# The value product of 16 meta keys: two native fp32 passes against one fp32r product over three stacked 16-row blocks

## The chip, the cores and the metric

The program runs on one core of one Trainium2 chip. The metric is the device time of one execution in microseconds (us); lower is better. TensorE (PE) multiplies, with PEld its weight load; VectorE (DVE), ScalarE (ACT) and GpSimd (POOL) work beside it; SyncE (SP) issues most DMAs. Engines tell each other of finished work by semaphores.

## The reference, cut to what matters

Two transformer blocks follow each other. The change is in the second block, in its two attentions. There 16 learned "meta" tokens stand before 1024 real tokens, so that every query sees 1040 keys.

```python
def second_block(x, meta_tokens, ...):
    h = concatenate([meta_tokens (16 rows), x (1024 rows)])
    z = rms_norm(h) @ w_in                      # qa ka va qb kb vb ga gb
    # A: 8 heads, each of two 64-wide score maps and 128-wide values
    w = softmax(q1 k1^T/8 + alibi) - lam * softmax(q2 k2^T/8 + alibi)
    oa = rms_norm(w @ va)
    # B: 8 query heads over 2 key heads, width 128, rotary positions
    ob = softmax(qh kh^T / sqrt(128)) @ vb
    h = h + (sigmoid(ga) * (oa @ wa) + sigmoid(gb) * (ob @ wb)) @ w_out
    # then 16 experts, each picking its top tokens, and a final norm
```

## The kernel before, in words

**Precision.** Large products are done in split form: each float32 operand is cut into a high part (a copy to the type fp32r) and a low part (operand minus high part, again fp32r), and three fp32r products hi·hi, hi·lo, lo·hi are added. Products with the probabilities are done natively in float32; a native product shows as two MATMUL records, each with its own weight load.

**Tiles.** Queries are taken 128 at a time: eight tiles (t = 0 to 7) of real tokens and a ninth (t = 8) for the 16 meta queries; in B the ninth holds the meta queries of four heads (64 rows). A has 8 × 9 = 72 tiles, B has `NB` = 66 (only the last head of each group has a ninth tile). For one tile:
- PE makes the scores against the 1024 real keys; DVE turns them into biased scores with a row maximum (TENSOR_TENSOR_REDUCE, shown as CUSTOM_DVE_ANT_0; L2579 in A, twice a tile for the two score maps; L2739 in B). The 16 meta scores were made earlier and are only copied in (L2576, L2737).
- ACT exponentiates the row of 1040 (L2176, L2341).
- DVE combines the two maps in A (L2595, "combine") or divides in B (L2746, L2748).
- PE turns the probabilities (L621): first the block of the 16 meta keys into the upper rows' place of bank 7, then the eight blocks of real keys into banks 5 and 6. ACT copies the first out (L2184 in A, L2396 in B) and then the eight (L2189, L2398).
- PE multiplies with the values: eight products over 128 real keys each (L3101, L3298), and one for the meta keys (L3102, L3299). For this last one the 16 rows of probabilities and of values lie in tiles of 128 rows whose other 112 rows are zero, and the product is native like the eight. ACT (L2195) or DVE (L2754, `result_b`) takes the result.

**Order in A.** The order is written out by hand on every engine. In step t of head h PE does: scores of tile t+1; half a unit of the next head's projections (L3037, 12 fp32r products of 348 columns); the turn of tile t; the other half unit; the value products of tile t-1. A unit is one third of the columns of the next head's keys, queries or values (`UNITS`), and the list runs k0 k1 k2 q0 q1 v0 v1 q2 v2 over t = 0 to 8. PE begins unit t+1 only when the results of unit t are out of their bank: for keys that is DVE's `lower_keys` (L2541, L2542). At t = 0 PE turns the head's values (L621 on vTa) after the value products, and it waits there for ACT's copy L2189 of tile 0, which frees banks 5 and 6. At t = 5 and t = 8 the meta scores of the next head follow the value products (L3050). The last head has no units beside it. In a step ACT does: result of tile t-2, exp of map 0, square, copy of the meta block, exp of map 1, copy of the eight blocks, unit.

**Order in B.** In step s PE does: scores of tile s+2 (L3263), half a unit if the step has one (t = 0 to 2 in most heads), the turn of tile s, the other half, the value products of tile s-1. PE turns tile s only when DVE has taken result s-2 out of bank 7. ACT does: meta copy, copy of the eight blocks, exp of tile s+2, unit, and at t = 4 and 5 the high part of the next head's queries (L2332), which DVE follows with the low part (L2716) at the end of its step. At t = 6 of a group's last head the next group's keys are split (L2327, L2729), and the next scores wait for them.

**Weights.** POOL splits each weight tile into its high part (CAST, L655) and low part (TENSOR_TENSOR, L657), started by PE's last use of the slot.

Of the kernel before, what the change touches and what calls it, by code (L numbers as in the profile page):

```python
# [13 lines left out]
P = 128  # L14
# [3 lines left out]
META = 16  # L18
# [104 lines left out]
CREDIT = 1  # L123

# [40 lines left out]
def build(nc, A, out):  # L165

    ctx = ExitStack()
    with ctx:
# [140 lines left out]
        ka_lo[1] = o.put("ka_lo1", [P, TP], F32R)  # L309
        tok_at = (top - 4 * (NT + 1) * D) // 32 * 32  # L310
# [8 lines left out]
        Va_meta = [o.put(f"Va_meta{j}", [P, P]) for j in range(2)]  # L319
        EA = [o.put(f"EA{j}", [P, T2]) for j in range(2)]  # L320
        EA2 = o.put("EA2", [P, T2])
        PTa = [o.put(f"PTa{j}", [P, NT + 1, P]) for j in range(2)]
# [23 lines left out]
        Vb_meta = [o.put(f"Vb_meta{j}", [P, HB]) for j in range(2)]  # L346
        PTb = [o.put(f"PTb{j}", [P, NT + 1, P]) for j in range(2)]
# [86 lines left out]
        def thirds(t):  # L434
# [28 lines left out]
            aa_bias aa_u aa_v aa_vf aa_qs aa_ql aa_kh aa_kl aa_vs aa_s aa_mt aa_ms aa_max aa_e aa_sm aa_c  # L463
# [4 lines left out]
            lg_z lg_c lg_y router_step lg_e lg_t hr_t hr_c tk_step tk_t tk_c  # L468
# [1463 lines left out]
        with nc.Block() as block:  # L1932

            @block.sync
# [205 lines left out]
            def _(act):  # L2140
# [69 lines left out]
                def head(h, odd, first=False, last=False):  # L2210

                    for t in range(NT + 1):
# [6 lines left out]
                        if t == 0:  # L2219
                            act.wait_ge(S["aa_v"], 3 * h + 1)  # L2220
                            act.activation(Va_meta[odd][0:META, :], bank(6, P, 0, META), ACT.Copy).then_inc(S["aa_vs"], 1)
# [160 lines left out]
                for s, (g, j, t) in enumerate(B_TILES):  # L2382
                    m = rows_of(t)
                    after = next_head(g, j)
                    if t == 0 and j == 0:
                        act.wait_ge(S["ob_v"], 3 * g + 1)
                        act.activation(Vb_meta[g][0:META, :], bank(6, P, 0, META), ACT.Copy).then_inc(S["ob_vs"], 1)
# [55 lines left out]
                act.activation(aff[:, :, 0:NE], aff[:, :, 0:NE], ACT.Exp).then_inc(S["lg_e"], 1)  # L2443
# [75 lines left out]
            def _(dve):  # L2519
# [229 lines left out]

                def result_b(s):  # L2750
# [33 lines left out]
                for zeros in (*(t[:, NT, :] for t in PTb), *(t[:, :] for t in Vb_meta)):  # L2784
                    dve.memset(zeros, 0.0).then_inc(S["bb_z"], 1)
                scores_b(1)
                divide(0)
                for s, (g, j, t) in enumerate(B_TILES):
                    after = next_head(g, j)
                    if t == 5 and after:  # L2790
# [62 lines left out]
                dve.wait_ge(S["lg_y"], 1)  # L2853
# [10 lines left out]
                dve.wait_ge(S["lg_e"], 1)  # L2864
# [155 lines left out]
            def _(pe):  # L3020
# [51 lines left out]
                def turn_probs(h, par, t, fresh, more=True):  # L3072
# [8 lines left out]
                    if t == 0:  # L3081
                        pe.wait_ge(S["aa_vs"], 3 * h + 1)
                        pe.wait_ge(S["aa_ms"], 6 * h + 6)
                    if t == 1:
                        pe.wait_ge(S["aa_vs"], 3 * h + 3)
# [10 lines left out]
                def values(h, odd, t, done):  # L3096
# [5 lines left out]
                    mm(bank(7, P, 0, m), PTa[par][:, NT, 0:m], Va_meta[odd][:, :], start=False, stop=True).then_inc(S["aa_o"], 1)  # L3102
# [163 lines left out]
                def turn_probs_b(s):  # L3266
# [11 lines left out]
                    if j == 0 and t < 2:  # L3278
                        pe.wait_ge(S["ob_vs"], 3 * g + (3 if t else 1))
# [10 lines left out]
                def values_b(s):  # L3290
# [3 lines left out]
                    if j == 0 and t == 0:  # L3294
                        pe.wait_ge(S["ob_vs"], 3 * g + 3)
# [3 lines left out]
                    mm(bank(7, m), Vb_meta[g][:, :], PTb[s % 2][:, NT, 0:m], start=False, stop=True).then_inc(S["bb_o"], 1)  # L3299
# [109 lines left out]
                last.then_inc(S["lg_y"], 1)  # L3409
# [157 lines left out]
```

## Time and profile before

| | |
|---|---|
| three runs | 3375.02, 3373.60, 3371.13 us; median 3373.6 |
| profiled execution | span 3371.0 us, 51781 instructions |
| busy | PE 3208.9 us (95%), DVE 1661.5 (49%), ACT 1123.6 (33%), POOL 991.2 (29%) |
| attention A | about 1338 to 1951 us |
| attention B | about 2181 to 2617 us |

The span runs from the first to the last instruction of the profiled execution; the page gives no other time for that execution, and the median of the runs is 2.6 us above it. A row of a timeline gives start, duration, engine, line, operation, tiles, shape and count; a bracket at its end is the idle time of the engine before it and what released it. PE records overlap: the pitch of equal matmuls is (duration of the row − duration of one) / (count − 1).

### The profile page before, as it was taken

How to read it: one execution, taken by the hardware profiler on the slowest of the kernel's cores; microseconds unless marked ns; L12 is line 12 of the kernel's file. 1: busy time of each engine (PE TensorE's matmuls, PEld its weight loads, DVE VectorE, ACT ScalarE, POOL GpSimd, SP SyncE). 2: the span in 40 equal slices, each digit the busy share in tenths (PEclk: the TensorE clock that was granted, in tenths of full speed). 3: DMA queues.
4: the chain of work that ended last, by engine and by line, in shares of the span. 5: the costliest groups of instructions: out<-in, count | busy, mean ns of one | idle time of the engine just before them, and what ended most of it. 6: DMA issues, size and time to landing. Idle time of an engine off the chain costs nothing.

```text
span 3371.0 us, 51781 instructions
## 1 busy us (share of the span) xinstructions
PE 3208.9 (95%) x20325; PEld 2832.4 (84%) x20325; DVE 1661.5 (49%) x2806; ACT 1123.6 (33%) x2092; POOL 991.2 (29%) x672
## 2 busy tenths in 40 slices
PE   7999989899999998999999899999999999789997
PEld 5677767688888877898989799998999999689997
DVE  5555556755554545666666623255455043522223
ACT  3433333333322223555555621155455110300002
POOL 3112224777772333222222133200000222012221
PEclk9999999999999998999999999999999999889998
DMA  4001112122234112000000012100000221468888
GB/s 156 26 32 32 32 63 100 63 75 75 79 108 176 50 53 79 20 26 20 20 20 20 14 44 82 65 25 26 24 22 20 79 90 57 176 224 308 316 306 293
DMA packets 80577, 294.90 MB, mean 87 GB/s; under 512 B 11298, under 2 KB 16226, under 8 KB 77200
## 3 DMA queue, kind: packets, MB, share of 16 engines
q1 hardware_dynamic: 67296, 243.92, 20.4%
q10 hardware_dynamic: 6944, 29.90, 2.2%
q0 software_dynamic: 6160, 18.63, 2.2%
q8 instruction: 122, 2.00, 0.2%
q14 instruction: 55, 0.45, 0.0%
HBM read 239.39 MB, written 47.70 MB: 85 GB/s over the span
## 4 chain that ended last, share of the span: by engine, by line
PE 55%; DVE 3%; issue 2%; ACT 2%; DMA 0%; POOL 0%; SPq 0%; POOLq 0%; DVEq 0%; ACTq 0%
PE PS L633 14%; PE PS L3037 7%; PE PS L3459 7%; PE PS L621 5%; PE PS L3222 4%; PE PS L3489 3%; PE PS L3101 3%; PE PS L3068 3%; PE PS L3298 3%; PE PS L3263 2%; PE PS L3102 0%; PE PS L3050 0%; PE PS L3235 0%; DVE where L2889 0%; DVE affT L2892 0%
## 5 line engine op out<-in xcount | busy, mean ns | idle before, releaser
L655 POOL CAST w_hi<-ring 128x1024 fp32r<-128x1024 f32 x130 | 135.7, 1044 | 1544.6 <-PE PS L633 434.3
L657 POOL TENSOR_TENSOR w_lo<-ring,w_hi 128x1024 fp32r<-128x1024 f32 x130 | 333.0, 2562 | 10.5
L2176 ACT ACTIVATE EA<-EA,small_sb 128x1040 f32<-128x1040 f32 x144 | 166.8, 1158 | 192.2 <-DVE small_sb L2579 192.0
L2579 DVE CUSTOM_DVE_ANT_0 EA<-PS,biasH,low_a 128x1024 f32<-128x1024 f32 x128 | 163.6, 1278 | 57.8 <-PE PS L3068 57.8
L3037 PE MATMUL PS<-u_hi,w_hi 128*128 128x348 f32 x504 | 173.5, 344 | 0.0
L3037 PE MATMUL PS<-u_lo,w_hi 128*128 128x348 f32 x504 | 162.1, 322 | 0.0
L3037 PE MATMUL PS<-u_hi,w_lo 128*128 128x348 f32 x504 | 161.8, 321 | 0.0
L1590 DVE TENSOR_TENSOR hid_lo<-hid,hid_hi 128x1024 fp32r<-128x1024 f32 x44 | 92.7, 2145 | 118.6 <-ACT hid_hi L1222 118.6
L1677 PE MATMUL PS<-u_hi,w_hi 128*128 128x512 f32 x352 | 147.1, 418 | 3.0 <-POOL w_lo L657 2.3
L1871 PE MATMUL PS<-t_hi,slot_hi 128*128 128x512 f32 x352 | 138.7, 394 | 9.4 <-DVE t_lo L1489 8.8
L3101 PE MATMUL PS<-Va,PTa 128*128 128x128 f32 (+1 forms) x1152 | 139.9, 275 | 0.0
L1677 PE MATMUL PS<-u_lo,w_hi 128*128 128x512 f32 x352 | 139.4, 396 | 0.0
L633 PE MATMUL PS<-u_hi,w_hi 128*128 128x348 f32 (+1 forms) x552 | 129.7, 339 | 10.0 <-DVE u_lo L584 3.9
L1677 PE MATMUL PS<-u_hi,w_lo 128*128 128x512 f32 x352 | 138.5, 394 | 0.0
L1871 PE MATMUL PS<-t_hi,slot_lo 128*128 128x512 f32 x352 | 138.5, 393 | 0.0
L1871 PE MATMUL PS<-t_lo,slot_hi 128*128 128x512 f32 x352 | 138.1, 392 | 0.0
L3101 PEld LDWEIGHTS PS<-Va,PTa 128*128 128x128 f32 (+1 forms) x1152 | 133.7, 181 | 3.1 <-issue 1.7
L3298 PE MATMUL PS<-PTb,Vb 128*128 128x128 f32 (+1 forms) x1056 | 128.8, 275 | 0.4 <-DVE obT L2754 0.4
L2595 DVE SCALAR_TENSOR_TENSOR EA<-EA,small_sb,EA 128x1040 f32<-128x1040 f32 (+1 forms) x72 | 127.1, 1765 | 2.5
L633 PE MATMUL PS<-u_lo,w_hi 128*128 128x348 f32 (+1 forms) x552 | 128.0, 335 | 0.0
L633 PE MATMUL PS<-u_hi,w_lo 128*128 128x348 f32 (+1 forms) x552 | 127.7, 335 | 0.0
L3459 PE MATMUL PS<-xsT,w_gate_sb 128*128 128x130 f32 x1024 | 126.9, 277 | 0.6 <-DVE xsT L2927 0.6
(485 smaller groups left out, 8256.6 us busy)
## 6 DMA issues: line engine op xcount, KB each, us to landing
ring<-in_stream SPq DMA_DIRECT2D x130, 512.0 KB, 3.5
w_gate_sb<-in_w_gate SPq DMA_DIRECT2D x64, 512.0 KB, 7.3
w_up_sb<-in_w_up SPq DMA_DIRECT2D x64, 512.0 KB, 8.2
w_down_sb<-in_w_down SPq DMA_DIRECT2D x64, 512.0 KB
gu_raw<-in_gate_up SPq DMA_DIRECT2D x22, 1024.0 KB, 5.4
hid_keep<-hid_out SPq DMA_DIRECT2D x17, 512.0 KB, 2.9
hid<-hid_keep ACTq DMA_DIRECT2D x15, 512.0 KB, 16.8
x_keep<-xT ACTq DMA_DIRECT2D x1, 4176.0 KB, 14.1
```

The source lines that it names most:

```text
L621: return nc.tensor.transpose(out, in_, eye[0:k, 0:k])
L633: last = mm(bank(to_bank, width), w[j][:, c, :], src[:, c, b * width:(b + 1) * width], start=(c == 0 and k == 0), stop=(c == KD - 1 and k ...
L655: pool.tensor_copy(w_hi[j][:, :, :], w_raw[j][:, :, :]).then_inc(S["w_rounded"], 1)
L657: pool.tensor_tensor(w_lo[j][:, :, :], w_raw[j][:, :, :], w_hi[j][:, :, :], ALU.subtract).then_inc(S["w_split"], 1)
L1677: last = mm(bank(2 + half), w[n % 2][:, d, :], src[:, d, half * BANK:(half + 1) * BANK], start=(d == 0 and k == 0), stop=(d == KD - 1 and ...
L1871: last = mm(product_bank(i, s), slots[s][w][:, c, :], operands[s][src][:, c, :], start=(c == 0 and k == 0), stop=(c == HALF - 1 and k == 2))
L2176: act.activation(e[0:m, :], e[0:m, :], ACT.Exp, scale=-1.0, bias=small[0:m, 8 + 2 * par + k:9 + 2 * par + k], accum_out=small[0:m, 12 + 2 ...
L2579: dve.tensor_tensor_reduce(e[0:m, 0:T1], wide(2 * k, T1, m), bias, -1.0, low_a[0:m, t, k:k + 1], ALU.add, ALU.min, low).then_inc(S["aa_max ...
L3037: last = mm(bank(WEAVE, CH), w[slot][:, d, :], src[:, d, columns_of(c)], start=(d == 0 and k == 0), stop=(d == KD - 1 and k == 2))
L3101: mm(bank(7, P, 0, m), PTa[par][:, j, 0:m], Va[:, j, :], start=(j == 0), stop=False)
L3298: mm(bank(7, m), Vb[:, i, :], PTb[s % 2][:, i, 0:m], start=(i == 0), stop=False)
L3459: last = mm(bank(b + 2 * (j % 2), CAP), w[:, j, c, :], xsT[:, c, :], start=(c == 0), stop=(c == KD - 1))
```

## The change

The meta part of the value product becomes one fp32r product. The 16 rows of probabilities p and of values v are cut into high and low parts, and three blocks of 16 rows are stacked at rows 0, 32 and 64 of tiles of 128 rows: the probabilities as (hi, lo, hi) and the values as (hi, hi, lo). One product over the stack is then hi·hi + lo·hi + hi·lo. The other rows stay zero.

- For each tile ACT copies the meta block to a 16-row tile of its own (`PTa_last`, `PTb_last`) and then twice more, SBUF to SBUF, into blocks 0 and 2; DVE subtracts to make block 1 (`lower_pt_meta`, `lower_pt_meta_b`).
- In A the first of the two copies stands before the exp of map 1 and waits for the copy out of PSUM just issued; the second stands behind that exp, before the copy of the eight blocks. DVE subtracts after the combine of tile t+1 and before the unit's low part.
- In B both copies stand behind the copy of the eight blocks and before the exp of tile s+2. DVE subtracts for tile s-1 at the start of step s, before meta scores, result and division.
- The values are split once a head in A (at t = 0: two ACT copies before the copy of the eight blocks, one DVE subtraction) and once a group in B.
- PE waits on two new semaphores (`mt_hi`, `mt_lo`) before the product. A few semaphores of the router stage are merged to make room.

```diff
+STACK = [slice(32 * n, 32 * n + META) for n in range(3)]
...
     def take_pt_meta(h, par, t, fresh):                        # ACT
...
-        act.activation(PTa[par][0:META, NT, 0:m], bank(7, m, P, META), ACT.Copy).then_inc(S["aa_pt"], 1)
+            act.wait_ge(S["mt_lo"], lowered(h, t - 2))
+        act.activation(PTa_last[par][:, 0:m], bank(7, m, P, META), ACT.Copy).then_inc(S["aa_pt"], 1)
+        act.wait_ge(S["aa_pt"], 18 * h + 2 * t + 1)
+        act.activation(PTa_meta[par][STACK[0], 0:m], PTa_last[par][:, 0:m], ACT.Copy).then_inc(S["mt_hi"], 1)
+
+    def repeat_pt_meta(par, t):
+        act.activation(PTa_meta[par][STACK[2], 0:m], PTa_last[par][:, 0:m], ACT.Copy).then_inc(S["mt_hi"], 1)
+
+    def split_meta_values(h, odd):
+        act.wait_ge(S["aa_vs"], 5 * h + 1)
+        for part in (0, 1):
+            act.activation(Va_meta[odd][STACK[part], :], Va_last[:, :], ACT.Copy).then_inc(S["aa_vs"], 1)
...
             exp(after[0], (after[1] + after[2]) % 2, after[2], 1)
+        repeat_pt_meta(par, t)
+        if t == 0:
+            split_meta_values(h, odd)
...
         take_pt(h, par, t)
...                                                             # ACT, B
         act.activation(PTb[s % 2][:, 0:NT, 0:m], ...)
+        for part in (0, 2):
+            act.activation(PTb_meta[s % 2][STACK[part], 0:m], PTb_last[s % 2][:, 0:m], ACT.Copy).then_inc(S["mt_hi"], 1)
         if s + 2 < NB:
             exp_b(s + 2)
...                                                             # DVE, A
+    def lower_pt_meta(h, par, t):
+        dve.wait_ge(S["mt_hi"], 18 * h + 2 * t + 1)
+        dve.tensor_tensor(PTa_meta[par][STACK[1], 0:m], PTa_last[par][:, 0:m], PTa_meta[par][STACK[0], 0:m], ALU.subtract).then_inc(S["mt_lo"], 1)
...
             attend(h, (odd + t + 1) % 2, t + 1, first)
+        lower_pt_meta(h, (odd + t) % 2, t)
+        if t == 0:
+            lower_meta_values(h, odd)
...                                                             # DVE, B
         for s, (g, j, t) in enumerate(B_TILES):
+            if s:
+                lower_pt_meta_b(s - 1)
...                                                             # PE, A (B likewise)
-        mm(bank(7, P, 0, m), PTa[par][:, NT, 0:m], Va_meta[odd][:, :], start=False, stop=True).then_inc(S["aa_o"], 1)
+        pe.wait_ge(S["mt_hi"], 18 * h + 2 * t + 2)
+        pe.wait_ge(S["mt_lo"], lowered(h, t))
+        mm(bank(7, P, 0, m), PTa_meta[par][:, 0:m], Va_meta[odd][:, :], start=False, stop=True).then_inc(S["aa_o"], 1)
```

## Rows read from the trace of the kernel before

**Rows 1.** Engines' busy time by stretch: A and B (start:end, length, then each engine).

```profile
1338.00:1951.00 613.00, 603.20 (x4496) 542.58 (x4495) 398.22 (x790) 335.51 (x742) 136.75 (x58) 1.00 0.06 19
2181.00:2617.00 436.00, 422.78 (x3056) 393.89 (x3054) 234.89 (x537) 222.85 (x371) 33.72 (x20) 1.00 0.08 23
```

**Rows 2.** PE's waits in B: total us, times, longest.

```profile
PE PS L621 <- DVE small_sb L2746: 7.8, 13, 1.2
```

**Rows 3.** Groups by line and shape: count, busy us, mean ns, idle before.

```profile
L3102 PE MATMUL PS<-Va_meta,PTa 128*128 128x128 f32 x128 | 24.7, 275 | 0.0
L3037 PEld LDWEIGHTS PS<-u_lo,w_hi 128*128 128x128 f32 x488 | 92.0, 189 | 0.0
L3101 PEld LDWEIGHTS PS<-Va,PTa 128*128 128x128 f32 x1024 | 121.9, 192 | 0.0
```

**Rows 4.** Timeline of PE at the end of an ordinary step of A.

```profile
1603.90 1.95 PE L3101 MATMUL PS<-Va,PTa 128*128 128x128 f32 x16
...
1605.68 0.39 PE L3102 MATMUL PS<-Va_meta,PTa 128*128 128x128 f32 x2
1606.00 0.30 PEld L3068 LDWEIGHTS PS<-ka_hi,qa_hi 64*128 64x128 f32 x4
...
1607.03 0.63 PE L3068 MATMUL PS<-ka_hi,qa_lo 64*128 64x512 f32 x4
1607.58 0.42 PE L3037 MATMUL PS<-u_hi,w_hi 128*128 128x348 f32 x1
```

**Rows 5.** Timeline of PE in B: native products with only 16 moving columns.

```profile
2266.88 1.86 PE L3246 MATMUL PS<-k_meta,q_f 128*128 128x16 f32 x16
```

**Rows 6.** ScalarE copies from SBUF to SBUF, by shape.

```profile
L2332 ACT ACTIVATE q_hi<-q_f 128x400 fp32r<-128x400 f32 x7 | 3.7, 528 | 0.0
L2335 ACT ACTIVATE qm_hi<-qm_f x2: 244/246/249, 2338.3 to 2569.9; 128x64 fp32r<-128x64 f32 x2
```

**Rows 7.** Timeline at the start (t = 0) of a head of A.

```profile
1647.66 0.27 ACT L2184 ACTIVATE PTa<-PS 16x128 f32<-16x128 f32 x1
1647.83 1.15 ACT L2176 ACTIVATE EA<-EA,small_sb 128x1040 f32<-128x1040 f32 x1
...
1648.98 1.00 ACT L2189 ACTIVATE PTa<-PS 128x1024 f32<-128x1024 f32 x1
...
1650.54 1.09 PE L621 MATMUL PS<-eye_sb,vTa 128*128 128x128 f32 x8
```

**Rows 8.** Timeline of DVE beside GpSimd at t = 7 of A.

```profile
1632.07 3.71 POOL L657 TENSOR_TENSOR w_lo<-ring,w_hi 128x1024 fp32r<-128x1024 f32 x1
...
1633.00 0.50 DVE L2546 TENSOR_TENSOR qa_lo<-qTa,qa_hi 128x348 fp32r<-128x348 f32 x1
1633.43 2.37 DVE L2576 COPY EA<-meta_a 128x16 f32<-128x16 f32 x1
```

**Rows 9.** Timeline at t = 2 of A: key split, then PE's next unit.

```profile
1589.51 0.52 DVE L2542 TENSOR_TENSOR ka_lo<-PS,ka_hi 128x348 fp32r<-128x348 f32 x1
...
1590.41 0.42 PE L3037 MATMUL PS<-u_hi,w_hi 128*128 128x348 f32 x1
```

**Rows 10.** Timeline of the last head of A: PE's turns of two neighbouring tiles.

```profile
1906.04 1.15 PE L621 MATMUL PS<-eye_sb,EA 128*16 128x128 f32 x9 [1.09 <-DVE EA L2595]
...
1911.87 1.15 PE L621 MATMUL PS<-eye_sb,EA 128*16 128x128 f32 x9 [1.09 <-DVE EA L2595]
```

**Rows 11.** Timeline of B at t = 4 to 6: query split and PE's turns.

```profile
2269.32 0.82 DVE L2716 TENSOR_TENSOR q_lo<-q_f,q_hi 128x640 fp32r<-128x640 f32 x1 [3.56 <-ACT q_hi L2332]
...
2271.14 1.19 PE L621 MATMUL PS<-eye_sb,EB 128*16 128x128 f32 x9 [0.91 <-DVE small_sb L2746]
...
2275.92 1.14 PE L621 MATMUL PS<-eye_sb,EB 128*16 128x128 f32 x9 [0.17 <-DVE small_sb L2746]
```

**Rows 12.** Timeline of B before the second group's keys.

```profile
2403.50 0.57 DVE L2716 TENSOR_TENSOR q_lo<-q_f,q_hi 128x400 fp32r<-128x400 f32 x1 [4.20 <-ACT q_hi L2332]
2403.69 2.64 POOL L657 TENSOR_TENSOR w_lo<-ring,w_hi 128x1024 fp32r<-128x1024 f32 x1
```

More of the change, by code:

```diff
@@ L309, in build @@
         ka_lo[1] = o.put("ka_lo1", [P, TP], F32R)
+        Va_last = o.put("Va_last", [META, P])
+        PTa_last = [o.put(f"PTa_last{j}", [META, P]) for j in range(2)]
         tok_at = (top - 4 * (NT + 1) * D) // 32 * 32
@@ L318, in build @@
         Va = o.put("Va", [P, NT, P])
-        Va_meta = [o.put(f"Va_meta{j}", [P, P]) for j in range(2)]
+        Va_meta = [o.put(f"Va_meta{j}", [P, P], F32R) for j in range(2)]
         EA = [o.put(f"EA{j}", [P, T2]) for j in range(2)]
         EA2 = o.put("EA2", [P, T2])
-        PTa = [o.put(f"PTa{j}", [P, NT + 1, P]) for j in range(2)]
+        PTa = [o.put(f"PTa{j}", [P, NT, P]) for j in range(2)]
+        PTa_meta = [o.put(f"PTa_meta{j}", [P, P], F32R) for j in range(2)]
         probs_end = o.at
@@ L345, in build @@
         qm_hi, qm_lo = (o.put(n, [P, GROUP * META], F32R) for n in ("qm_hi", "qm_lo"))
-        Vb_meta = [o.put(f"Vb_meta{j}", [P, HB]) for j in range(2)]
-        PTb = [o.put(f"PTb{j}", [P, NT + 1, P]) for j in range(2)]
+        Vb_meta = [o.put(f"Vb_meta{j}", [P, HB], F32R) for j in range(2)]
+        Vb_last = o.put("Vb_last", [META, HB])
+        PTb = [o.put(f"PTb{j}", [P, NT, P]) for j in range(2)]
+        PTb_meta = [o.put(f"PTb_meta{j}", [P, P], F32R) for j in range(2)]
+        PTb_last = [o.put(f"PTb_last{j}", [META, P]) for j in range(2)]
         assert o.at <= early_at
@@ L1932, in build, with lowered, lowered_b @@
         with nc.Block() as block:
+            def lowered(h, t):
+                return (NT + 2) * h + t + (2 if t > 0 else 1)
+            def lowered_b(s):
+                return LOWERED_A + s + 1 + sum(B_TILES.index((g, 0, 0)) < s for g in range(KV))
             @block.sync
@@ L2220, in head @@
                             act.wait_ge(S["aa_v"], 3 * h + 1)
-                            act.activation(Va_meta[odd][0:META, :], bank(6, P, 0, META), ACT.Copy).then_inc(S["aa_vs"], 1)
+                            if not first:
+                                act.wait_ge(S["mt_lo"], lowered(h - 1, 0) + 1)
+                            act.activation(Va_last[:, :], bank(6, P, 0, META), ACT.Copy).then_inc(S["aa_vs"], 1)
                         after = (h, odd, t + 1) if t < NT else None if last else (h + 1, 1 - odd, 0)
@@ L2789, in _ @@
                     after = next_head(g, j)
+                    if s:
+                        lower_pt_meta_b(s - 1)
+                    if t == 1 and j == 0:
+                        lower_meta_values_b(g)
                     if t == 5 and after:
@@ L3298, in values_b @@
                         mm(bank(7, m), Vb[:, i, :], PTb[s % 2][:, i, 0:m], start=(i == 0), stop=False)
[L3299 removed]
+                    if t == 0 and j == 0:
+                        pe.wait_ge(S["mt_lo"], lowered_b(s) + 1)
+                    pe.wait_ge(S["mt_hi"], SPLIT_A + 2 * s + 2)
+                    pe.wait_ge(S["mt_lo"], lowered_b(s))
+                    mm(bank(7, m), Vb_meta[g][:, :], PTb_meta[s % 2][:, 0:m], start=False, stop=True).then_inc(S["bb_o"], 1)
                 def whole_unit(g, x, c, b):
```

61 lines of the change are left out of this document (43 added, 18 removed).

## The prediction

> **What bounds the kernel.** I read the busy shares of two stretches first. In attention A PE is busy 603 of 613 us and in B 423 of 436 [rows 1]; DVE and ACT are busy about half. So a nanosecond taken from PE counts nearly everywhere, and one added to DVE or ACT counts only where PE waits for a chain of them. Those places are what decides, since the change takes from PE and gives to both others. The waits name them: 13 turns in B wait for DVE, 7.8 us together [rows 2]; the last head of A, which has no projections beside it, has a wait of 1.09 us in each step [rows 10]. A third kind has no wait yet, only a thin margin: the start of a head in A [rows 7].
>
> **What PE saves.** The product stands once in each of 72 + 66 = 138 tiles as two MATMULs [rows 3]. Sixteen such records take 1.95 us, one 0.275, so the pitch is (1.95 − 0.275) / 15 = 0.112 us [rows 4]. Does the one fp32r MATMUL fit into less than a pitch? Its 128 columns at the full clock are 0.053 us, but its neighbour's weights must be in. Sixteen products with only 16 moving columns still have a pitch of (1.86 − 0.26) / 15 = 0.107 us [rows 5], so a load of 128 columns alone costs that, and an fp32r load takes 189 ns where a native one takes 192 [rows 3], so it isn't quicker. I take 2 × 0.112 before, 0.112 after: 0.112 us saved.
>
> In six of nine steps of a head in A the next product is a score of 64 rows. Its load waits until the array is empty: the last meta record starts at 1605.68 + 0.39 − 0.275 = 1605.80, the load at 1606.00, 0.20 later, which is 0.107 of streaming and 0.10 of emptying [rows 4]. (The other way round it is the same: last score 1607.27, next load 1607.58, 0.213 of streaming and 0.10.) There the shorter streaming counts too: 0.112 + 0.107 − 0.053 = about 0.16 us saved. In the three other steps native products or turns follow: 0.112.
>
> - A: seven heads with PE the bound, 6 × 0.16 + 3 × 0.112 = 1.31 us each (the first lacks one product of 0.112): 9.05. Last head: 0.2, at its end.
> - B: 66 tiles less the 14 in which a chain sets the step (below): 52 × 0.112 = 5.8.
> - Together 15.1 us.
>
> Bounds of one product: 0.168 saved, if only its columns counted; 0 if its 128 fp32r columns took as long as the two native records, since the narrowest fp32r product in the trace has 344 to 348 columns, as on L3037 [rows 4] and nothing shows 128. I take 0.112 to 0.16, near the loads.
> The Trainium skill ("TensorE: Matmul & The Clock Gate", Back-to-back issue gap) gives N/2.4 + 2.5 ns as the gap of warm matmuls, 56 ns here; by it each product would save 0.168 us and PE 23 us at most in 138. The row with 16 columns, at 107 ns, speaks against it.
>
> **What the others gain.** ACT has no row for a 16x128 copy from SBUF. 64 columns take 0.246 and 400 take 0.528 [rows 6]: 0.84 ns a column, 0.30 us for 128. Back to back ACT's copies overlap by about 0.09, so each costs 0.21; bounds 0.17, the start-to-start of a copy out of PSUM [rows 7], and 0.30 without overlap. The copy that waits for the one before it loses that overlap: exp of map 1 starts 0.17 after the meta copy now [rows 7], and then 0.27 + 0.03 + 0.21 = 0.51 after it, 0.34 later. DVE's subtraction: 348 columns have a start-to-start of 0.43 [rows 8]; 220 fewer at 1.04 ns make 0.20. Bounds 0.1 and 0.29 (a lone small copy; no overlap).
>
> **A, ordinary steps.** The exp of map 1 comes 0.34 later and so does the combine, the copy of the eight blocks 0.55. PE needs the combine nearly 4 us after it ends, and the copy 4 to 5 us. Hidden. So are the new waits before the product: its parts are made a step earlier. Memsets and renamed semaphores cost nothing.
>
> **A, t = 0.** PE wants to turn the head's values and needs the copy of the eight blocks. That copy ends at 1649.98, PE comes at 1650.54: a margin of 0.5 with the semaphore [rows 7]. Before it ACT now has 0.34 + 0.21 (probabilities) + 0.42 (values) = 0.97 more, and DVE's subtraction of the tile before shifts the chain by 0.1. PE comes 0.19 earlier by its own savings. Stall: 0.97 + 0.1 − 0.5 + 0.19 = 0.75. Heads 1 to 6: 4.5 us. First and last head wait there already, and only 0.63 (the first copy falls in a wait) and 0.73 are added. Together 5.9.
>
> **A, t = 2.** The last third of the key split ends at 1589.51 + 0.52 = 1590.03; PE starts its next unit at 1590.41 [rows 9]. The subtraction stands before that split: 0.20 later, PE 0.16 earlier, so about 0.03 a head, 0.2 in all.
>
> **A, last head.** Steps are 5.83 us apart, and each turn waits 1.09 us for DVE's combine [rows 10]. DVE (two score passes, reciprocals, combine) and the exp between are a closed loop, the subtraction stands in it, and ACT's first copy falls in ACT's wait for DVE. 7 × 0.21 = 1.5 us, with PE's saving worth nothing there.
>
> **B, ordinary steps.** Both copies stand behind the copy of the eight blocks, so the exp of tile s+2 comes 0.42 later. The loop of exp (1.3 us with its accumulator), division (0.95), meta copy and score pass (1.5) and the passing on between engines (0.25) is 4.0 us; a step of PE without a unit is about 4.4 (4.78 between the turns of rows 11, its wait included), one with a unit nearly 4 us more. Hidden. DVE's subtraction falls in its wait for PE.
>
> **B, t = 4 and 5.** In five heads PE waits 0.91 and 0.17 us for a result that stands on DVE behind the low part of the queries, which waits for ACT's high part, which stands behind exp [rows 11]. All that is serial: two copies 0.42 and the subtraction 0.20 = 0.62 a turn, in 10 turns 6.2 us, and these steps lose the saving (it is not counted above). In the third head key roots make two such steps more: 0.4 in all.
>
> **B, before the second group.** The low part of the queries starts at 2403.50, POOL's subtraction at 2403.69 [rows 12]. With 0.42 on ACT it starts at 2403.92, behind POOL. What then happens is seen where a small DVE copy came behind POOL: 2.37 us instead of 0.17 [rows 8]. DVE's next division was held there anyway until 2406.1, so about 1.2 us of it reaches the scores that wait for the split keys. Two steps.
> Losses: 5.9 + 0.2 + 1.5 + 6.2 + 0.4 + 1.2 = 15.4.
>
> **Sum.** 15.4 − 15.1 = +0.3 us: the profiled span would be 3371.3 for 3371.0, and with the 2.6 us between that span and the median, 3373.9. What the change saves on PE it gives back in about 30 steps.
>
> **Rivals.**
> 1. *An fp32r product of 128 columns is no faster than the native pair.* For: no row has one; every product in this kernel with 130 columns or fewer is native. Against: fp32r with 348 columns streams one column per clock. Place: the 138 products; it decides once the MATMUL takes 0.21 us instead of 0.053. Then the 15.1 us go, the stalls at t = 0 are 0.19 shorter (7 × 0.19 = 1.3), and 3373.9 + 15.1 − 1.3 = 3387.7. Chance 0.22.
> 2. *DVE's subtraction loses its port to POOL at t = 2 of A.* The row at 1633.43 shows a DVE copy held for POOL's whole operation, while the subtraction at 1633.00, right behind a combine, wasn't held [rows 8]. The new one stands right behind the combine as well, so I think it keeps its place. If not, the key split and PE's unit wait 2.2 us in seven heads: +15, 3389. Chance 0.05.
> The Trainium skill ("SBUF — State Buffer", SBUF: two separate sides) says that the pair of ports which DVE and GpSimd share is an exclusive lock, taken also by a DVE operation with two SBUF inputs, and that whichever starts first keeps it for the whole instruction. The copy of 2.37 us agrees.
> 3. *The chains give way.* If ACT's copies cost 0.17 and overlap waits that I count as critical, or the head start has more slack than one head shows, losses halve: 3366. If none reached PE, 3358.8. For: most of ACT's and DVE's time is idle. Against: each place has its wait or its margin of under 0.6 us in the trace. Chance 0.18.
> 4. *The load isn't the limit.* 0.056 more in some 67 products: −3.8, 3370. Chance 0.07, within the forecast's range.
>
> **Chances.** Forecast 0.48, rivals 0.22, 0.05, 0.18, 0.07. A measurement of this kernel can tell about 0.2%, 6.7 us, from no change. Rivals 1 and 2 are slower; of the forecast's own case (3368 to 3380, as the copies cost 0.17 or 0.30) a little is on either side; half of rival 3 and more is faster. Faster 0.19, same 0.51, slower 0.30. The range runs from half the losses to the top of rival 1: 3365 to 3389.
>
> **What would show it.** One MATMUL of 0.112 pitch at the product's line, with the next score load 0.15 us after it starts; a record of about 0.43 us there would be rival 1. PE waiting for the copy of the eight blocks before it turns a head's values, 0.5 to 0.8 us in each head. Last head's steps at 6.0 us. In B, the waits at t = 5 and 6 grown by about 0.6, and ordinary steps 0.11 shorter. A subtraction of over 2 us on DVE beside POOL would be rival 2. I am wrong if the head's turn waits for nothing, or if the ordinary steps don't get shorter.

## The result, and the profile after

The changed kernel takes 3406.1 us (median of 4 runs, 3402.4 to 3410.3), the kernel before 3373.5 beside it: ratio 1.0096, interval 1.0084 to 1.0107, about 32 us slower. The forecast of 3373.9 and its range miss it. The profiled spans are 3401.5 and 3371.0 us.

Where the 30.5 us of the spans lie is seen from the starts of PE's turns of probabilities. From the first to the last turn of A it was 611.1 us and is 635.9, in B 429.0 and 435.6; A is 24.8 longer, B 6.6, and the rest 0.9 shorter. The two stretches after:

```profile
1324.00:1991.00 667.00, 627.51 (x4626) 564.10 (x4622) 434.76 (x897) 406.36 (x926) 142.11 (x63) 0.99 0.06 19
2205.00:2647.00 442.00, 418.25 (x2989) 389.95 (x2988) 256.68 (x605) 261.06 (x507) 32.98 (x19) 0.99 0.08 23
```

In A PE now stands still for 39 us; in the kernel before it was 10.6 between 1324 and 1966 us (9.8 in the somewhat shorter stretch of [rows 1]). Its waits there, and below them those in B (total us, times, longest), which answer to [rows 2]:

```profile
PE PS L3106 <- DVE ka_lo L2585: 16.4, 7, 2.4
PE PS L629 <- ACT o_tok L2223: 10.3, 6, 1.8
PE PS L629 <- ACT PTa L2217: 9.0, 7, 3.4
...
PE PS L629 <- DVE small_sb L2801: 17.8, 11, 2.0
PE PS L3337 <- DVE k_lo L2784: 3.3, 1, 3.3
```

The first line is new and the largest: seven times, once a head, PE waits for the low part of the next head's keys before its unit L3106. The timeline of DVE, POOL and PE there (t = 2 of head 4; the last row answers to the second of [rows 9]):

```profile
1680.28 1.76 DVE L2638 SCALAR_TENSOR_TENSOR EA<-EA,small_sb,EA 128x1040 f32<-128x1040 f32 x1
...
1681.02 3.25 POOL L665 TENSOR_TENSOR w_lo<-ring,w_hi 128x1024 fp32r<-128x1024 f32 x1
...
1682.07 2.35 DVE L2648 TENSOR_TENSOR PTa_meta<-PTa_last,PTa_meta 16x128 fp32r<-16x128 f32 x1
...
1684.45 0.38 DVE L2584 COPY kmeta<-PS 64x16 f32<-64x16 f32 x2
1684.86 0.52 DVE L2585 TENSOR_TENSOR ka_lo<-PS,ka_hi 128x348 fp32r<-128x348 f32 x1
...
1685.52 0.40 PE L3106 MATMUL PS<-u_hi,w_hi 128*128 128x348 f32 x1 [2.36 <-DVE ka_lo L2585]
```

The added subtraction (L2648) needs 0.28 us elsewhere and takes 2.35 here: it ends 0.15 after POOL's subtraction. POOL had its own row open since 1681.02, held by the combine L2638, and went first when that ended.

The same place in the kernel before, with the split L2542 of [rows 9] between its last two rows:

```profile
1587.07 2.12 DVE L2595 SCALAR_TENSOR_TENSOR EA<-EA,small_sb,EA 128x1040 f32<-128x1040 f32 x1
...
1588.18 3.26 POOL L657 TENSOR_TENSOR w_lo<-ring,w_hi 128x1024 fp32r<-128x1024 f32 x1
...
1589.12 0.37 DVE L2541 COPY kmeta<-PS 64x16 f32<-64x16 f32 x2
...
1589.95 1.53 DVE L2576 COPY EA<-meta_a 128x16 f32<-128x16 f32 x1
```

POOL's row was open here too, until 1591.44. The two copies and the split, which read from PSUM, were not held (0.37 for two, 0.52). The first operation behind them that reads only SBUF, the copy L2576, was: 1.53 us instead of 0.17, until 1591.48. So the hold was already there, behind what PE waits for. The subtraction, with both inputs in SBUF, brought it in front of that.

In two of the seven heads something comes on top. PE's clock by stretch in head 2 (the number after POOL's count is the granted clock, 1.00 = 2.4 GHz, 0.50 = 1.2 GHz):

```profile
1518.00:1520.00 2.00, 1.12 (x7) 1.15 (x8) 1.97 (x6) 0.00 (x0) 0.00 (x0) 1.00 0.55 137
1520.00:1521.50 1.50, 1.50 (x7) 1.40 (x6) 1.29 (x5) 1.46 (x4) 0.00 (x0) 0.50 0.41 167
1521.50:1523.00 1.50, 1.50 (x8) 1.45 (x7) 0.00 (x0) 1.01 (x4) 0.00 (x0) 0.50 0.00 0
1523.00:1525.00 2.00, 2.00 (x14) 2.00 (x13) 1.02 (x4) 1.95 (x4) 0.00 (x0) 0.89 0.00 0
```

PE had been idle for 2.35 us until 1518.88; about 1.1 us later it runs at half speed, for 3.4 us (the second and third stretch, and the start of the fourth). That costs 1.6 us more in this head (a step of 11.50 and one of 9.34 us, where head 1 has 10.82 and 8.41).

The next lines show the rest of A: the last head (the turn of t = 3), where each turn came 5.83 us after the one before [rows 10] and now comes 6.27 after it.

```profile
1927.70 1.30 DVE L2638 SCALAR_TENSOR_TENSOR EA<-EA,small_sb,EA 128x1040 f32<-128x1040 f32 x1
...
1929.03 0.28 DVE L2648 TENSOR_TENSOR PTa_meta<-PTa_last,PTa_meta 16x128 fp32r<-16x128 f32 x1
1929.24 1.14 PE L629 MATMUL PS<-eye_sb,EA 128*16 128x128 f32 x9 [1.69 <-ACT o_tok L2223]
1929.34 0.17 DVE L2619 COPY EA<-meta_a 128x16 f32<-128x16 f32 x1
1929.43 1.28 DVE L2622 CUSTOM_DVE_ANT_0 EA<-PS,biasH,low_a 128x1024 f32<-128x1024 f32 x1
```

From combine to the next score pass it is now 1.73 us; without the subtraction it was 1.30. So the subtraction costs 0.43 in a chain, though its row is 0.28 long: it begins 0.03 after its predecessor's end and lets the next begin 0.03 after its own, while DVE's other neighbours overlap by 0.07 to 0.1 us (L2619 and L2622 here), an overlap of 0.08 that is lost too.

The start of a head, which answers to [rows 7]:

```profile
1659.79 0.27 ACT L2201 ACTIVATE PTa_last<-PS 16x128 f32<-16x128 f32 x1
1660.08 0.31 ACT L2203 ACTIVATE PTa_meta<-PTa_last 16x128 fp32r<-16x128 f32 x1
1660.30 1.15 ACT L2192 ACTIVATE EA<-EA,small_sb 128x1040 f32<-128x1040 f32 x1
1661.36 0.18 ACT L2192 ACTIVATION_READ_ACCUMULATOR EA<-EA,small_sb 128x1 f32 x1
1661.57 0.31 ACT L2207 ACTIVATE PTa_meta<-PTa_last 16x128 fp32r<-16x128 f32 x1
1661.90 0.64 ACT L2212 ACTIVATE Va_meta<-Va_last 16x128 fp32r<-16x128 f32 x2
1662.56 1.02 ACT L2217 ACTIVATE PTa<-PS 128x1024 f32<-128x1024 f32 x1
```

From the meta copy to the copy of the eight blocks it was 1.32 us; it is 2.77. And B, the turn at t = 5, which answers to the first two of [rows 11]:

```profile
2290.87 0.62 ACT L2437 ACTIVATE PTb_meta<-PTb_last 16x128 fp32r<-16x128 f32 x2
...
2294.72 0.83 DVE L2771 TENSOR_TENSOR q_lo<-q_f,q_hi 128x640 fp32r<-128x640 f32 x1 [4.08 <-ACT q_hi L2365]
2295.58 0.28 DVE L2812 TENSOR_TENSOR PTb_meta<-PTb_last,PTb_meta 16x128 fp32r<-16x128 f32 x1
...
2296.98 1.19 PE L629 MATMUL PS<-eye_sb,EB 128*16 128x128 f32 x9 [1.99 <-DVE small_sb L2801]
```

From q_lo to the turn it was 1.82 us and is 2.26, again 0.44 for one subtraction. The step before the second group, which answers to [rows 12]:

```profile
2429.78 2.39 POOL L665 TENSOR_TENSOR w_lo<-ring,w_hi 128x1024 fp32r<-128x1024 f32 x1
...
2430.24 2.35 DVE L2771 TENSOR_TENSOR q_lo<-q_f,q_hi 128x400 fp32r<-128x400 f32 x1 [4.05 <-ACT q_hi L2365]
```

Here q_lo has come behind POOL, as foretold, and takes 2.35 us for 0.57.

### The profile page after: what moved, and what is told of

It is laid out like the page before. It is cut to its first block, busy times and chain, and to the rows that moved or that the text cites. A ratio compares the mean times of both kernels' runs of the same rounds, so it can differ in the third digit from the quotient of the medians.

```text
span 3401.5 us, 52164 instructions
## 1 busy us (share of the span) xinstructions
PE 3200.3 (94%) x20187; PEld 2824.7 (83%) x20187; DVE 1699.8 (50%) x2954; ACT 1218.3 (36%) x2388; POOL 988.5 (29%) x672
## 3 DMA queue, kind: packets, MB, share of 16 engines
q1 hardware_dynamic: 67296, 243.92, 20.5%
## 4 chain that ended last, share of the span: by engine, by line
PE 47%; DVE 6%; ACT 4%; issue 3%; DMA 1%; POOL 0%; SPq 0%; ACTq 0%; POOLq 0%; DVEq 0%
PE PS L641 14%; PE PS L3537 6%; PE PS L3106 5%; PE PS L629 5%; PE PS L3372 3%; PE PS L3296 3%; PE PS L3567 3%; PE PS L3337 2%; PE PS L3137 2%; PE PS L3170 2%; DVE EA L2638 1%; ACT EA L2192 1%; DVE EA L2622 1%; DVE PTa_meta L2648 1%; DMA fin<-h_rows 0%
## 5 line engine op out<-in xcount | busy, mean ns | idle before, releaser
L3106 PE MATMUL PS<-u_hi,w_hi 128*128 128x348 f32 x504 | 173.8, 345 | 16.4 <-DVE ka_lo L2585 16.4
L2622 DVE CUSTOM_DVE_ANT_0 EA<-PS,biasH,low_a 128x1024 f32<-128x1024 f32 x128 | 163.9, 1280 | 46.8 <-PE PS L3137 46.8
L3106 PE MATMUL PS<-u_lo,w_hi 128*128 128x348 f32 x504 | 162.8, 323 | 0.0
L3106 PE MATMUL PS<-u_hi,w_lo 128*128 128x348 f32 x504 | 162.4, 322 | 0.0
L2504 ACT ACTIVATE silu_e<-PS 128x130 f32<-128x130 f32 x64 | 18.0, 280 | 324.7 <-PE PS L3537 322.7
L3372 PEld LDWEIGHTS PS<-PTb,Vb 128*128 128x128 f32 x1056 | 128.1, 197 | 0.7 <-DVE obT L2818 0.5
```

The costliest lines, as they stand in the source:

```text
L2622: dve.tensor_tensor_reduce(e[0:m, 0:T1], wide(2 * k, T1, m), bias, -1.0, low_a[0:m, t, k:k + 1], ALU.add, ALU.min, low).then_inc(S["aa_max ...
L3106: last = mm(bank(WEAVE, CH), w[slot][:, d, :], src[:, d, columns_of(c)], start=(d == 0 and k == 0), stop=(d == KD - 1 and k == 2))
L3372: mm(bank(7, m), Vb[:, i, :], PTb[s % 2][:, i, 0:m], start=(i == 0), stop=False)
```

## The experiments

The table gives the pitch of PE's turns of probabilities (us from the start of one tile's turn to that of the next), read from the profile of every kernel: what one place costs is seen without the noise of the whole. Heads of A are 0 to 7; "t = 0", "t = 2" and "t = 8" are the steps that begin with that tile's turn, in head 1 (head 2 in brackets where it differs); "last" is a step in the middle of head 7; B's are the steps up to the turns of t = 5 and t = 6 and one without a unit. A and B are the times from the first to the last turn.

| kernel | t=0 | t=2 | t=8 | last | B t=5 | B t=6 | B plain | A | B |
|---|---|---|---|---|---|---|---|---|---|
| before | 9.66 | 8.59 | 9.09 | 5.83 | 7.25 | 4.77 | 4.39 | 611.1 | 429.0 |
| changed | 10.63 | 10.82 (11.50) | 9.42 | 6.27 | 8.21 | 5.87 | 4.28 | 635.9 | 435.6 |
| product_only | 9.49 | 8.46 | 9.09 | 5.83 | 7.25 | 4.78 | 4.28 | 602.0 | 426.5 |
| sub_behind_split | 10.61 | 8.46 | 9.41 | 6.26 | 8.21 | 6.24 | 4.28 | 615.4 | 439.5 |
| sub_before_combine | 10.62 | 8.45 | 9.12 | 5.83 | 8.21 | 5.96 | 4.28 | 611.5 | 436.9 |
| sub_at_zero_2 | 10.51 | 10.71 | 9.31 | 6.02 | 7.97 | 5.62 | 4.27 | 630.6 | 434.7 |
| a_start | 9.49 | 8.47 | 9.11 | 5.83 | 8.21 | 5.96 | 4.27 | 602.6 | 437.0 |
| b_order | 10.61 | 10.82 (11.58) | 9.42 | 6.27 | 7.34 | 4.82 | 4.28 | 635.8 | 425.6 |
| both_orders | 9.49 | 8.46 | 9.12 | 5.83 | 7.35 | 4.82 | 4.28 | 601.0 | 427.1 |

B as a whole varies by 4 us between profiles of the same order (435.6, 436.9, 437.0, 439.5), so for it the single steps count. Part of this is the clock: in every profile the granted clock is 0.50 for some stretches of B, together 3.4 us in the kernel before, 10.2 in the changed one and in product_only, 13.7 in sub_behind_split. The last has it at 0.50 from 2420 to 2424 us, a fall that the profile of the changed kernel doesn't have at this place.

The kernel before was timed beside each group of runs: its median is 3373.9 us beside the first three experiments and 3375.3 beside sub_at_zero_2, a_start, b_order and both_orders, so differences in time between the groups carry 1 to 2 us of their own.

### product_only: the fp32r product without its operands' cost

```
-  act.activation(PTa[par][0:META, NT, 0:m], bank(7, m, P, META), ACT.Copy)
+  act.activation(PTa_meta[par][0:META, 0:m], bank(7, m, P, META), ACT.Copy)       # PTa_meta, Va_meta: F32R
-  mm(bank(7, P, 0, m), PTa[par][:, NT, 0:m], Va_meta[odd][:, :], start=False, stop=True)
+  mm(bank(7, P, 0, m), PTa_meta[par][:, 0:m], Va_meta[odd][:, :], start=False, stop=True)   # B likewise
```

> The kernel before with one change: the product of the meta keys is one fp32r MATMUL over 128 rows, of which only the first 16 hold values (written once, rounded, by the ACT copy that is there anyway); no split copies and no subtractions, so the low parts are left out of this product. My theory: each product saves 0.112 us, 0.16 us where a score follows in A; all of it reaches the end, 15.1 us, so 3373.5 - 15.1 = 3358 (0.9955 of before). Ordinary steps of a head in A 8.58 -> 8.42, a B step without a unit 4.39 -> 4.28. Rival: the product saves nothing, or what it saves is lost at the waits that are already there: 3370 to 3373.

Measured: 3359.7 us (3359.1 to 3361.0), ratio to before 0.9958, interval 0.9944 to 0.9972: 14.2 us faster. Ordinary steps of A (t = 1 to 7) fall by 0.10 to 0.18, plain steps of B by 0.11, and the steps that wait in the kernel before (last head, B t = 5 and 6) don't move. The gain per product was sized rightly, and the rival of a slow fp32r product is out. Between this kernel and the changed one lie 43.9 us of span, A 33.9, B 9.0 and 1.0 elsewhere: what ACT's copies and DVE's subtractions cost.

### sub_behind_split and sub_before_combine: the same subtraction in another place

```
   # sub_behind_split                               # sub_before_combine
-  lower_pt_meta(h, (odd + t) % 2, t)               scores(h, par, t, 0, fresh)
   ...                                              scores(h, par, t, 1, fresh)
   lower_keys(h + 1, ...)  or lower_queries(...)  +  lower_pt_meta(*behind)        # the tile before
+  lower_pt_meta(h, (odd + t) % 2, t)               combine(h, par, t, fresh)
```

> The changed kernel, in A DVE's subtraction (and that of the values) moved behind the low part of the next head's keys or queries. Theory (port): the subtraction stands directly behind the combine while POOL's subtraction of the weights is pending, POOL goes first, and the key split behind it comes 2.4 us late in seven heads; in two of them the granted clock falls to 0.50 for some 3 us after that idle time, 1.6 us more each. So the seven waits of PE for ka_lo go, the step from t=2 to t=3 falls from 10.82 to about 8.45, and the time by 7 x 2.4 + 2 x 1.6 = 20 us: 3386 (0.994 of the changed kernel). Rival (ACT): the key split is late because ACT's two copies stand before the high part of the keys; then the move brings only DVE's 0.3 us in each of seven heads: 3404.

Measured: 3389.4 us (3384.5 to 3391.8), ratio to before 1.0050, interval 1.0033 to 1.0067: 16.6 less than the changed kernel. The step of t = 2 falls from 10.82 to 8.46, in heads 2 and 5 from 11.5 and 9.3 to 8.4 and 8.4, and A is 20.5 us shorter, as the port theory has it. ACT's copies stand where they stood, so they were not what held the keys. The other 4 us went back in B, where the clock is at 0.50 for 3.4 us more than in the changed kernel's profile.

> The changed kernel, in A the subtraction of tile t moved ahead of the combine of tile t+1, where DVE waits 2.2 us for the exp of map 1. Port theory: the seven stalls of 2.4 us and the two falls of the clock go (20 us), and in the last head the subtraction leaves the closed loop: 7 x 0.43 = 3 us, steps from 6.27 to 5.85; at t=0 the chain is shorter by 0.4 in heads 1 to 7, 2.5 us. Together 25 us: 3380. Rival (ACT's copies set the last head's steps and the start of each head): only the stall at t=2 goes, 3386.

Measured: 3381.6 us (3379.0 to 3388.2), ratio 1.0027, interval 1.0015 to 1.0038: 24.4 less than the changed kernel for 25 expected. The last head is back at 5.83 and t = 8 at 9.12, so both had only the subtraction in their way. But t = 0 stays at 10.62: there it is ACT alone. That part of the expectation, 2.5 us, was wrong, and 11.67 to 11.23 in the last head's first step is all that came of it.

### sub_at_zero_2: the same subtraction, its result at partition 0

```
-  dve.tensor_tensor(PTa_meta[par][STACK[1], 0:m], PTa_last[par][:, 0:m], PTa_meta[par][STACK[0], 0:m], ALU.subtract)
+  dve.tensor_tensor(PTa_meta[par][STACK[0], 0:m], PTa_last[par][:, 0:m], PTa_meta[par][STACK[0], 0:m], ALU.subtract)   # B likewise
```

> The changed kernel, only the subtraction of the probabilities (in A and in B) writes its result over the first block of 16 rows, at partition 0, and not into the second, at partition 32; the low part of the probabilities and one of the two high parts are thereby left out of the product. Same instruction, same place, same size. Theory (offset): an operation that touches a partition other than 0 begins 0.03 us after its predecessor has ended and not 0.07 before, and in that gap POOL takes the port. Then the subtraction now keeps its place as qa_lo does: no 2.35 us row at t=2, the time falls by about 20 us there; last head's steps 6.27 -> 6.17 (0.7 us), the turns at t=5 and 6 in B 0.1 to 0.2 us earlier each (1.5 us): 3384. Rival (size): it is the 16 partitions or the small size that make it lose; the 2.35 us rows stay and the time is 3405.

A first form, sub_at_zero, gave the result tiles of its own; they did not fit into SBUF, and it has no time. In this one block 0 ends up with the low part and block 1 stays zero. So what is left out of the product is hi·hi, and not the low part, as the expectation has it; the work of each engine is the same.

Measured: 3400.7 us (3399.5 to 3401.4), 5.4 less than the changed kernel. Neither theory holds as written. Timelines of DVE and POOL beside the combine of a ninth tile (16 rows) and of a fourth tile (128 rows):

```profile
1479.10 1.81 DVE L2638 SCALAR_TENSOR_TENSOR EA<-EA,small_sb,EA 16x1040 f32<-16x1040 f32 x1
...
1479.91 3.92 POOL L665 TENSOR_TENSOR w_lo<-ring,w_hi 128x1024 fp32r<-128x1024 f32 x1
...
1480.84 0.27 DVE L2648 TENSOR_TENSOR PTa_meta<-PTa_last,PTa_meta 16x128 fp32r<-16x128 f32 x1
1481.04 0.50 DVE L2589 TENSOR_TENSOR qa_lo<-qTa,qa_hi 128x348 fp32r<-128x348 f32 x1
...
1598.09 1.78 DVE L2638 SCALAR_TENSOR_TENSOR EA<-EA,small_sb,EA 128x1040 f32<-128x1040 f32 x1
1599.79 2.45 DVE L2648 TENSOR_TENSOR PTa_meta<-PTa_last,PTa_meta 16x128 fp32r<-16x128 f32 x1
```

The subtraction now begins 0.07 to 0.08 before the combine's end, and where it stands in a chain alone the step is 0.24 to 0.25 us shorter (last head 6.27 to 6.02, B t = 5 8.21 to 7.97): so much does writing at partition 32 cost beyond the row itself. The result now also overwrites one of its inputs, a second difference; the probes of the next section write elsewhere and begin 0.07 to 0.08 before the combine's end as well, so it is the partition. Behind the 16-row combine it keeps the port; in the changed kernel it lost it there too:

```profile
1478.45 2.38 DVE L2648 TENSOR_TENSOR PTa_meta<-PTa_last,PTa_meta 16x128 fp32r<-16x128 f32 x1
```

Behind the 128-row combine, where PE's wait comes from, it loses either way. Offset decides the one place and not the other.

### shapes_behind_combine and wide_combine: who gets the port

```
   # shapes_behind_combine: t == 2 of heads 0 to 6, directly behind the combine; rows, n by head
+  SHAPES = ((16, 128), (128, 128), (128, 16), (16, 16), (64, 128), (128, 348), (16, 348))
+  dve.tensor_tensor(meta_a[0:rows, 0:4, :, :]...[:, 0:n], eye[0:rows, 0:n], ones[0:rows, 0:n], ALU.subtract)
```

> As sub_before_combine, with one more DVE subtraction put directly behind the combine at t=2 of heads 0 to 6 (two constant SBUF tiles, all at partition 0, the result to a place that nobody reads any more), in a new size per head: 16 rows x 128 columns, 128x128, 128x16, 16x16, 64x128, 128x348, 16x348. sub_at_zero_2 has shown that starting before the combine's end doesn't keep the port (2.45 us). Theory (number of elements per row): short operations lose it to POOL and long ones keep it: rows of 2.3 us for 16 and 128 columns whatever the partitions, 0.5 us for 348 columns with 128 and with 16 rows. Rival (partitions): 16 rows lose with 348 columns too, 128 rows keep it at every width. Rival (what stood before): none of the sizes matters, all seven lose or all seven keep it. PE's wait at t=2 stands only in heads that lose: 2.2 us each.

All seven lose (3398.9 us, one run). Groups of DVE by shape (mean ns before the last bar):

```profile
L2658 DVE TENSOR_TENSOR qa_lo<-eye_sb,ones_sb 128x348 fp32r<-128x348 f32 x1 | 2.7, 2682 | 0.0
...
L2656 DVE TENSOR_TENSOR meta_a<-eye_sb,ones_sb 128x128 f32<-128x128 f32 x1 | 2.5, 2454 | 0.0
L2656 DVE TENSOR_TENSOR meta_a<-eye_sb,ones_sb 16x128 f32<-16x128 f32 x1 | 2.5, 2450 | 0.0
...
L2656 DVE TENSOR_TENSOR meta_a<-eye_sb,ones_sb 16x16 f32<-16x16 f32 x1 | 2.3, 2331 | 0.0
```

Neither partitions nor columns save it: the third outcome, "none of the sizes matters". The step of t = 2 is back at 10.6 to 10.7 us in heads 0 to 4, the same 2.2 us, and is 11.3 and 12.2 in heads 5 and 6. What remains is what stood before, and that all of them, unlike the key split, read only SBUF.

```
   # wide_combine
   def combine(h, par, t, fresh):
-      m = P if t < NT else META
+      m = P
```

> As sub_before_combine, with the combine of the ninth tile (t=8, 16 rows) made over all 128 partitions; what it writes beyond row 15 is read by nobody. All seven probes behind a 128-row combine lost the port, while qa_lo behind the 16-row combine keeps it in every kernel so far (0.50 us). Theory (rows of the predecessor): behind a 128-row operation POOL goes first, behind a 16-row one DVE does; then qa_lo now takes 2.7 us in heads 0 to 6. Rival (the place: another engine's timing there, or POOL's own): qa_lo stays at 0.50 us and the copy behind it at 2.38. The time changes by less than 3 us either way, since what stands behind is held in either case: 3379 to 3385.

Measured: 3384.2 us, one run. DVE at step 7 of head 1:

```profile
1474.07 1.79 DVE L2638 SCALAR_TENSOR_TENSOR EA<-EA,small_sb,EA 128x1040 f32<-128x1040 f32 x1
1475.79 2.71 DVE L2589 TENSOR_TENSOR qa_lo<-qTa,qa_hi 128x348 fp32r<-128x348 f32 x1
```

Made 128 rows wide, the combine leaves the port to POOL, and qa_lo, 0.50 us in [rows 8], takes 2.71 or 2.72 in all seven heads. POOL's row begins 0.8 us after the combine's start in both cases, so its timing isn't the difference. So here the rows of the operation before decide. And [rows 8], on which I had relied, told only of a predecessor of 16 rows, in the kernel before:

```profile
1630.91 2.16 DVE L2595 SCALAR_TENSOR_TENSOR EA<-EA,small_sb,EA 16x1040 f32<-16x1040 f32 x1
```

### a_start, b_order and both_orders: the chains relieved

```
   # a_start (on sub_before_combine), ACT at t == 0
    take_pt_meta; exp; take_pt; take_unit
+   first_pt_meta(h, par, t); split_meta_values(h, odd, 0)
    the two copies of the values
+   repeat_pt_meta(par, t); split_meta_values(h, odd, 1)        # DVE's subtractions of t == 0 behind lower_keys
   # b_order (on the changed kernel), ACT
    act.activation(PTb_last[s % 2][:, 0:m], bank(7, m, P, META), ACT.Copy)
+   for part in (0, 2): act.activation(PTb_meta[s % 2][STACK[part], 0:m], PTb_last[s % 2][:, 0:m], ACT.Copy)
    act.activation(PTb[s % 2][:, 0:NT, 0:m], ...)
-   for part in (0, 2): ...
   # b_order, DVE at t in (4, 5)
+   lower_pt_meta_b(s)
    lower_queries(*after, t - EARLY + 1)
```

> As sub_before_combine (3381.6), and at t=0 of a head in A the split copies of ACT (probabilities and values) stand behind the copy of the eight blocks and the one of the keys' high part: two ahead of the two copies of the values and two behind them; DVE's subtractions of t=0 stand behind the low part of the keys. Theory: the step of t=0 is 1.13 us longer than with the fp32r product alone (10.62 for 9.49) only because PE waits for the copy of the eight blocks; it falls to 9.5 in heads 0 to 6 and from 11.23 to about 10.0 in the last: 7 x 1.13 + 1.2 + 0.2 = 9.3 us, 3372.3. Rival: the delayed copies of the values and PE's next turn take part of it back: half, 3377.

Measured: 3373.0 us (3368.5 to 3377.1), ratio 0.9991, interval 0.9982 to 1.0000. The step of t = 0 is 9.49 again, the last head's first 10.21. A is 9.0 us shorter than in sub_before_combine (9.3 expected); the values' copies took nothing back.

> The changed kernel, only B's order changed: ACT makes the two split copies of the probabilities between the copy of the meta columns and that of the eight blocks, where it idles 0.6 us, and in the tiles t=4 and 5 DVE subtracts ahead of the low part of the queries, where it idles 4 us. Theory: the turns of t=5 and 6 are late (8.21 and 5.95 us where the fp32r product alone has 7.25 and 4.78) because 0.5 to 0.6 us of copies and 0.43 us of subtraction stand in a serial chain. With both out of it the steps come back to 7.35 and 4.85: 5 x 2.0 = 10 us, 3406 - 10 = 3396. Rival (ACT's time counts wherever it stands): the copies now delay the copy of the eight blocks and exp as before, only the 0.43 of DVE goes: 5 x 0.86 = 4.3, 3402.

Measured: 3393.8 us (3392.2 to 3395.4), ratio 1.0054, interval 1.0039 to 1.0069: 12.2 less than the changed kernel, B 10.0 less in the profile. Timeline of ACT and DVE up to the turn of t = 5 and what follows it:

```profile
2292.25 0.82 DVE L2771 TENSOR_TENSOR q_lo<-q_f,q_hi 128x640 fp32r<-128x640 f32 x1 [3.33 <-ACT q_hi L2365]
...
2294.07 1.19 PE L629 MATMUL PS<-eye_sb,EB 128*16 128x128 f32 x9 [1.13 <-DVE small_sb L2801]
2294.38 0.27 ACT L2432 ACTIVATE PTb_last<-PS 16x128 f32<-16x128 f32 x1 [2.16 <-PE PS L629]
2294.68 0.64 ACT L2435 ACTIVATE PTb_meta<-PTb_last 16x128 fp32r<-16x128 f32 x2
```

From q_lo to the turn it is 1.82 us again; the two copies fill the idle 0.6 us of ACT. The step before the second group gained as well, which the expectation doesn't have: q_lo now starts ahead of POOL's subtraction there and takes 0.58 us, and the step is 6.12 us for 7.94.

> The orders of a_start and b_order in one kernel; it computes all that the changed kernel does. If the costs add: 3381.6 - 9.3 - 10 = 3362.3, within 3 us of the fp32r product alone (3359.7), and 0.9966 of the kernel before. If both rivals hold: 3373, no change from before.

Measured: 3359.3 us (3356.7 to 3360.7), ratio to before 0.9950, interval 0.9937 to 0.9964: faster than both kernels, by 16 us than the one before it was run beside and by 47 than the changed one. It does the changed kernel's whole arithmetic and is as fast as the fp32r product without its operands' cost. PE's waits in A:

```profile
PE PS L629 <- ACT o_tok L2228: 8.0, 7, 1.3
PE PS L629 <- ACT PTa L2222: 2.3, 1, 2.3
```

The wait for ka_lo is gone, that for the eight blocks stands once instead of seven times.

## Why the prediction was wrong, point by point

- **PE's saving, 15.1 us: right per product, in the sum partly by luck.** product_only has 14.2 (interval 9.4 to 18.9), and in its profile 13.4. Of these, 9.1 are in A, for 9.05 worked out, but only 2.5 in B, for 5.8, where the clock is at 0.50 for 6.8 us more than in the kernel before, which is up to 3.4 us; 1.8 came from outside A and B, where nothing was changed for it.
- **A, t = 2, 0.2 us: the step that failed.** It cost 20.0 us: 2.4 in five heads, 4.0 in heads 2 and 5, with the fall of the clock. It was rival 2, which I gave 0.05, with its mechanism, its place and its 2.2 us; the clock was not in it. The argument against it, that "the new one stands right behind the combine as well", took two differences for none: the witness followed a combine of 16 rows, and it touched partition 0 only. wide_combine and sub_at_zero_2 show one each, and at t = 2 the first alone decides. The trace of the kernel before had the hold at this very place, on the copy at 1589.95.
- **The subtraction in a chain, 0.20 us: a term too small by half.** It is 0.43. I took the start-to-start of an operation that overlaps its neighbours; this one doesn't, and has 0.28, a gap of 0.03 on either side and 0.08 of overlap lost, 0.42. At partition 0 it would have been right: in sub_at_zero_2 the last head's steps are 6.02, 0.19 above 5.83. It made the last head's steps 0.44 longer for 0.21 (2.2 us in all for 1.5), and 0.3 in six steps from t = 8, which I had not counted (1.9 us).
- **ACT's copies, 0.21 each: too small.** Their pitch is 0.31 to 0.33. That is the upper bound that I had worked out, 0.30, but I chose by a pair of copies that overlap.
- **A, t = 0: right place, 0.75 predicted, 1.14 measured** against product_only; with the last head 9.8 us for 5.9. The chain grew by 1.45, for 0.97.
- **B, t = 4 and 5: right place, 0.62 a turn predicted, 0.96 and about 1.1 measured**, 10.3 us in five heads for 6.2. In the third head the two steps cost 0.45 each (7.79 to 8.24 and 6.60 to 7.04 us), 0.9 for 0.4.
- **B, before the second group: right place and mechanism, 1.2 predicted, 1.8 measured** (7.94 for 6.12). The rest of B still came out 1.3 below product_only: that profile has falls of the clock in steps where PE is the bound (among them the two behind this one, 8.53 and 5.28 there, 7.80 and 4.36 in the changed kernel), which no part of the prediction had.
- **Ordinary steps hidden: right.** Those of A are 0.10 to 0.18 us shorter than before and those of B 0.11, with all copies and subtractions beside them.

Sum of the losses: 43.9 for 15.4. Of the 28.5 that were missing, 19.8 are the port and the clock at t = 2, 8.7 all the rest: mostly the sizes of copies and subtraction and what they made of each chain, and 1.0 outside A and B. With the rest alone the forecast would have been 3382.6, inside the range; the port took it out. (In rival 3 the time without any loss is 3373.9 − 15.4 = 3358.5 and not 3358.8.)

The Trainium skill ("SBUF — State Buffer", SBUF: two separate sides) has the lock, and held. It gives the pair to whichever operation starts first, and POOL's row starts first in all these cases; that DVE keeps it behind a 16-row combine and loses it behind a 128-row one doesn't follow from that, only from the runs.

## What to carry to other kernels

A small operation on an engine that is half idle is priced by what stands behind it in the queue: here 0.28 us of DVE became 2.4 us of PE, and moving the line by one place took it away. Before trusting a row as a witness, compare all of its neighbourhood, the size of the operation before and the partitions touched too, and give the case that it excludes more than one chance in twenty. When the product saves what it should and the time rises, don't undo the change: find the idle stretch of each engine and put the preparation there; the same arithmetic went from 32 us slower to 16 us faster.

## What the runs showed of the hardware

- **A subtraction that writes at another partition than its neighbours doesn't overlap them.** The one that writes 16 rows at partition 32 starts 0.03 us after its predecessor, and the next one, all at partition 0, 0.03 after it. Writing at partition 0 it starts 0.07 before the predecessor's end, and a chain is 0.25 us shorter (sub_at_zero_2). ACT's copy to partition 64 shows the same gap (1661.57 after 1661.54 above), but that was not tried by itself.
- **Who gets the port behind an operation that holds it** depends on that operation's rows: behind a combine of 128 rows a waiting POOL operation went first for every DVE operation tried that reads only SBUF (2.33 to 2.72 us, seven sizes of the probe and qa_lo), behind one of 16 rows DVE kept it if it overlapped. DVE's operations with an input in PSUM (L2541, L2542) were not held behind 128 rows either. Why the rows matter is open.
- **One idle stretch can halve PE's clock.** After a wait of 2.35 us the granted clock fell to 0.50 for 3.4 us in two of seven equal cases, heads 2 and 5, in the changed kernel and in the same two in b_order, and in head 4 alone in sub_at_zero_2; it cost about 1.6 us each. Why not in all seven is open.
- **One fp32r MATMUL in place of a native pair of 128 columns** takes 0.11 us off a plain step of B, as the pitch of the native products with 16 columns [rows 5] had let expect, and 0.13 to 0.18 off the steps of A in which products of 64 rows follow it.
